# The two value blocks of a group put side by side behind the scores, over one stretch of a hybrid-attention decoder step

## The chip, the cores and the metric

The kernel runs on one core of a Trainium2 chip. The metric is the device time of one execution in microseconds, and the median of three executions stands for a kernel.

## What is computed

One decoder layer for 512 prompt tokens and for 8 sample sequences of 8 new tokens each. The part that matters here is the attention of the samples over stored keys and values: differential attention over 4096 paged positions in 4 heads, and dilated window attention over a stored window of 2048 positions in 8 heads.

```python
qa, ka, va, qb, kb, vb = _project(_rms_norm(xs, norm_attn_g[l]), w_in[l], pos_s)
k_past = cache_k_diff[l][page_table].reshape(db, PAST_LEN, N_HEADS_DIFF, 2, HEAD_DIM)
v_past = cache_v_diff[l][page_table].reshape(db, PAST_LEN, N_HEADS_DIFF, DIFF_V_DIM)
oa = _diff_attention_sample(qa, ka, va, k_past, v_past, lam)
ob, k_win, v_win = _dilated_attention_sample(qb, kb, vb, state_k_win[l], state_v_win[l])
...
s_past = jnp.einsum('bqhcd,bkhcd->bchqk', q, k_past, preferred_element_type=jnp.float32) * SCALE
p = jax.nn.softmax(jnp.concatenate([s_past, s_new], axis=-1), axis=-1)
w = p[:, 0] - lam * p[:, 1]
o = (jnp.einsum('bhqk,bkhe->bqhe', w[..., :p_len], v_past.astype(jnp.float32))
     + jnp.einsum('bhqk,bkhe->bqhe', w[..., p_len:], v_new.astype(jnp.float32)))
```

## The kernel before

The samples' attention is cut into 8 items of two sequences each. Items 0 to 3 read the paged cache, in 8 groups each; items 4 to 7 read the window state, in 3 groups each. That makes `KSLOTS` = 44 groups. A group is two halves (one for each sequence) of four pages of 128 keys; the third group of a state item has two pages a half. The program is one list of slots t = 0 to 52, each of eight steps i = 0 to 7, and every engine walks that list in its own program order. In slot t the keys of group t are scored, and the values of group t - 8 (`LAG` = 8) are weighed.

TensorE's part of a slot, before the change:

- i = 2: scores of half 0 (`score_keys`, line 1232, 16 matmuls into one PSUM bank);
- i = 4: turns the probabilities of group t - 8 (`turn_probs`, line 1245), which ScalarE then copies to `pt_sb` (line 1701); with the last group of an item also the scores of the new keys (line 1214);
- i = 5: values of half 0 (`weigh_values`, line 1270, 16 matmuls);
- i = 6: an item's new probabilities (line 1253) or its output (line 1329), then scores of half 1;
- i = 7: values of half 1, and an item's new values (line 1283).

Between these, each step has a share of the prompt's work (`pieces`): projection first, then the prompt's attention (lines 1084, 1099, 1115, 1132), and from slot 35 on the output projection (line 1189) with its transposes (line 1202). After slot 41 there is next to none of it until the prompt's second norm (line 1021).

VectorE transposes each key page from `k_ring` to `kt_sb` (`turn_page`, line 2175) once the scores of the page's half in the slot before have been made, and takes a slot's scores out of PSUM when both halves are there (`keep_scores`, line 2212). With an item's last group it then works out the bias (lines 2226 to 2243), and ScalarE makes the exponentials (line 1731). ScalarE also builds the next item's queries (`fetch_q`, lines 1686 and 1691), and for that it waits until all scores of the item before are made, half 1 of its last group included.

SyncE issues the loads in program order. `k_ring` holds one group of keys and `v_ring` one group of values. The load of value half h for slot t waits on `pv_half[h]`, which is the end of `weigh_values(t - 1, h)`. In SyncE's list the values of half 0 for slot t + 1 stand at i = 6 of slot t, one or two key loads behind them, and the values of half 1 at i = 0 of slot t + 1. From slot 44 on values go to three rings (`k_ring`, `v_ring`, `t_ring`), and ScalarE issues some of the loads.

Of the kernel before, what the change touches and what calls it, by code (L numbers as in the profile page):

```python
# [97 lines left out]
FIRST = [sum(QUADS[:it]) for it in range(ITEMS)]  # L98
KSLOTS = sum(QUADS)
# [7 lines left out]
def item_of(q):  # L107
    it = max(i for i in range(ITEMS) if FIRST[i] <= q)
    return it, q - FIRST[it]
# [7 lines left out]
def is_last(q):  # L117
    it, g = item_of(q)
    return g == QUADS[it] - 1


def has_k(t):
    return 0 <= t < KSLOTS


def has_v(t):
    return 0 <= t - LAG < KSLOTS
# [73 lines left out]
def pieces(t, i):  # L201
    return range(upto(t, i - 1), upto(t, i))
# [159 lines left out]
def build(nc, ins, outs):  # L362
    from contextlib import ExitStack
    ctx = ExitStack()
    with ctx:
# [643 lines left out]
        def _(pe):  # L1009
# [196 lines left out]
            def score_new_keys(it):  # L1206

                t0 = 4 * (it // 4)
                pe.wait_ge(rope_done, rope_no(8 if it < 4 else 20))
                pe.wait_ge(q_ready, it + 1)  # L1210
                if Z_NO["n", it]:
                    pe.wait_ge(z_free[1], Z_NO["n", it])
                for f in range(4):
                    last = nc.tensor.matmul(Z[1][32 * f:32 * f + 32, 0:NS], q_nat[:, f, :], k_s[:, t0 + f, :],
                                            start=True, stop=True)
                last.then_inc(z_full[1], 1)

            def score_keys(t, h):

                it, g = item_of(t)  # L1220
                n = pages_of(t)
                pe.wait_ge(kt_done, half_end(t, h))
                if g == 0:
                    pe.wait_ge(q_ready, it + 1)
                    pe.wait_ge(q_ready_dve, 1)
                if t and h == 0:
                    pe.wait_ge(s_evac, t)
                for r in range(4):
                    c0 = 32 * n * (2 * h + r // 2)
                    for f in range(4):  # L1230
                        c = 32 * (4 * f + r)
                        last = nc.tensor.matmul(S[32 * f:32 * f + 32, c0:c0 + 32 * n], q_st[:, h, f, r, :],  # L1232
                                                kt_sb[:, 4 * h:4 * h + n, c:c + 32], start=r % 2 == 0, stop=r % 2 == 1)
                last.then_inc(scored if h else half_scored, 1)

            def turn_probs(t):

                it, g = item_of(t - LAG)
                n = pages_of(t - LAG)
                pe.wait_ge(exp_done, EXP_NO[it, 4 * half_of(it, g) + 3] + 1)  # L1240
                if X_NO["p", t]:
                    pe.wait_ge(x_free, X_NO["p", t])
                for k in range(4):
                    c = col0(it, g) + 32 * n * k
                    last = nc.tensor.transpose(X[0:32 * n, k * P:(k + 1) * P], s_sb[:, c:c + 32 * n], ident[:, :])  # L1245
                last.then_inc(x_full, 1)

            def turn_new_probs(t):

                it = item_of(t - LAG)[0]  # L1250
                pe.wait_ge(exp_done, EXP_NO[it, 8] + 1)
                pe.wait_ge(x_free, X_NO["m", t])
                nc.tensor.transpose(X[0:NS, 0:P], s_sb[:, mini0(it):mini0(it) + NS], ident[:, :]).then_inc(x_full, 1)

            def weigh_values(t, h):

                q = t - LAG
                it, g = item_of(q)
                rows = 32 * pages_of(q)
                pe.wait_ge(x_free, X_NO["p", t] + 1)  # L1260
                if g == 0 and h == 0 and it:
                    pe.wait_ge(o_scaled, it)
                ring = ring_of(t)
                landed = (k_landed, v_landed, t_landed)[ring]
                for k in range(pages_of(q)):
                    pe.wait_ge(landed[4 * h + k], V_LANDS[q, 4 * h + k])
                for b in range(4):
                    values = (k_ring[0:rows, 4 * h + b, :], v_ring[0:rows, h, b, :], t_ring[0:rows, h, b, :])[ring]
                    for f in range(4):
                        last = nc.tensor.matmul(O[32 * f:32 * f + 32, P * h:P * h + P], pt_sb[0:rows, 4 * f + b, :],  # L1270
                                                values[:, f * P:(f + 1) * P],
                                                start=g == 0 and b == 0 and h == 0, stop=False, skip_group_check=True)
                last.then_inc(pv_half[h], 1)
# [51 lines left out]
            def turn_output(it):  # L1325

                pe.wait_ge(o_scaled, it + 1)
                pe.wait_ge(x_free, X_NO["o", it])
                nc.tensor.transpose(X[:, 0:P], o_row[:, :], ident[:, :]).then_inc(x_full, 1)
# [9 lines left out]
            for t in range(SLOTS):  # L1339
                for i in range(8):  # L1340
                    if i == 4 and has_v(t):
                        turn_probs(t)
                    if i == 4 and has_k(t) and is_last(t):
                        score_new_keys(item_of(t)[0])
                    if i == 6 and has_v(t) and is_last(t - LAG):
                        turn_new_probs(t)
                    if i == 6 and has_v(t - 1) and is_last(t - 1 - LAG):
                        turn_output(item_of(t - 1 - LAG)[0])
                    for p in pieces(t, i):
                        main(p)  # L1350
                    if i % 4 == 2 and has_k(t):
                        score_keys(t, i // 4)
                    if i == 5 and has_v(t):
                        weigh_values(t, 0)
                    if i == 7 and has_v(t):
                        weigh_values(t, 1)
                        if is_last(t - LAG):
                            weigh_new_values(t)
                    if (t, i) == (KSLOTS + 1, 6):

                        pe.wait_ge(ones_set, 1)
                        pe.wait_ge(sq_s_done, 1)
                        pe.wait_ge(z_free[1], Z_NO["s", 4])
                        nc.tensor.matmul(Z[1][:, 0:4 * NS], ones[:, :], sub_sq_s[:, :, :].rearrange("p g t -> p (g t)"),
                                         start=True, stop=True).then_inc(z_full[1], 1)
                    if (t, i) == (KSLOTS + 5, 4):
                        pe.wait_ge(norm_s_done, 1)
                        pe.wait_ge(z_free[1], len(Z_NO))
                        pe.wait_ge(wo_in, 16 * 8)
                        sample_out(0)  # L1370
# [1296 lines left out]
```

## Time and profile before

| | |
|---|---|
| median of three executions | 1108.67 us (1107.43 to 1110.65) |
| the profiled execution | 1107.77 us |
| its span | 1106.0 us |
| TensorE busy in the span | 960.3 us (87%) |
| VectorE, ScalarE busy | 671.5 us (61%), 506.3 us (46%) |
| mean granted TensorE clock | 0.949 of full speed |
| bytes moved | 310.98 MB, 281 GB/s on average |

The profile is of one execution. A line such as "L1270" is a line of the program; a matmul of float32 operands shows as two records, so the 16 matmuls of one half are "x32". PE is TensorE, DVE is VectorE, ACT is ScalarE, SPq is SyncE's queue of issues. What stands in square brackets is the idle time ahead of an instruction and what ended it.

### The profile page before, as it was taken

The numbers are of one execution on the slowest core, as the hardware profiler recorded it, in microseconds if no ns is written. First come the engines' busy times: TensorE is split into PE (matmuls) and PEld (weight loads), VectorE is DVE, ScalarE is ACT, GpSimd is POOL, SyncE is SP. The second block draws the span as 40 slices with busy tenths as digits, with TensorE's granted clock in tenths as the row PEclk, the third lists the DMA queues.
The fourth block names the chain that finished last, engine by engine and source line by source line (L and its number), as shares of the span: only waits on it lengthen the run. The fifth ranks groups of instructions, "written<-read, shape, count | busy, mean of one in ns | idle before, by whom it ended". The sixth has DMA issues, their size and how long they took to land.

```text
span 1106.0 us, 29349 instructions
## 1 busy us (share of the span) xinstructions
PE 960.3 (87%) x11050; PEld 852.3 (77%) x11050; DVE 671.5 (61%) x1632; ACT 506.3 (46%) x1118; POOL 133.9 (12%) x69
## 2 busy tenths in 40 slices
PE   3989898998777778888788757899999999999996
PEld 3978787887665556667566544699999999999996
DVE  5389655675458896765255444888888888800004
ACT  6554443373124656655144163465555555711124
POOL 1322211111000010001121000000000000043331
PEclk9989999999988998896999888999999999999998
DMA  8699999999999999978988699368676868956542
GB/s 252 240 310 341 326 317 356 367 351 334 299 323 335 348 353 336 323 229 275 328 284 298 197 301 255 130 252 317 256 311 248 319 245 311 324 176 235 192 166 86
DMA packets 174933, 310.98 MB, mean 281 GB/s; under 512 B 13601, under 2 KB 87714, under 8 KB 173282
## 3 DMA queue, kind: packets, MB, share of 16 engines
q1 hardware_dynamic: 172898, 305.24, 80.7%
q10 hardware_dynamic: 1920, 4.20, 1.4%
q8 instruction: 74, 1.21, 0.5%
q14 instruction: 41, 0.34, 0.1%
HBM read 302.30 MB, written 73.92 MB: 340 GB/s over the span
## 4 chain that ended last, share of the span: by engine, by line
PE 31%; issue 30%; SPq 13%; DMA 12%; DVE 7%; ACT 5%; ACTq 0%; POOL 0%; DVEq 0%; POOLq 0%
PE ps L1383 11%; SPq L666 7%; DMA v_ring<-in_cache_v_diff 6%; PE ps L1038 5%; SPq L768 4%; PE ps L1232 4%; PE ps L1270 4%; DVE kt_sb L2175 2%; PE ps L1189 2%; DMA k_ring<-in_state_v_win 2%; PE ps L1115 1%; SPq L756 1%; DMA k_ring<-in_cache_k_diff 1%; DMA k_ring<-in_state_k_win 1%; ACT q_st L1686 1%
## 5 line engine op out<-in xcount | busy, mean ns | idle before, releaser
L2175 DVE STREAM_TRANSPOSE kt_sb<-k_ring 128x512 f32<-128x512 f32 x336 | 221.2, 692 | 95.1 <-DMA k_ring<-in_cache_k_diff 41.7
L1270 PE MATMUL ps<-v_ring,pt_sb 128*32 128x128 f32 (+1 forms) x2496 | 93.6, 295 | 73.2 <-DMA v_ring<-in_cache_v_diff 59.6
L1270 PEld LDWEIGHTS ps<-v_ring,pt_sb 128*32 128x32 f32 (+1 forms) x2496 | 72.1, 117 | 88.8 <-issue 74.8
L1038 PE MATMUL ps<-h_hi,w_hi 128*128 128x288 f32 x384 | 125.1, 326 | 2.3 <-DVE h_lo L2028 2.3
L1038 PE MATMUL ps<-h_lo,w_hi 128*128 128x288 f32 x384 | 115.7, 301 | 0.0
L1038 PE MATMUL ps<-h_hi,w_lo 128*128 128x288 f32 x384 | 115.3, 300 | 0.0
L1232 PE MATMUL ps<-kt_sb,q_st 128*32 128x128 f32 (+1 forms) x2816 | 95.8, 279 | 9.5 <-DVE q_st L2185 4.6
L989 POOL TENSOR_TENSOR c_lo<-c_raw,c_hi 128x1408 fp32r<-128x1408 f32 x14 | 46.7, 3336 | 434.9 <-ACT c_hi L1789 434.9
L1232 PEld LDWEIGHTS ps<-kt_sb,q_st 128*32 128x32 f32 x2816 | 72.1, 113 | 26.8 <-issue 18.5
L1038 PEld LDWEIGHTS ps<-h_hi,w_hi 128*128 128x128 f32 x384 | 74.8, 195 | 16.4 <-issue 13.8
L949 POOL TENSOR_TENSOR w_lo<-w_raw,w_hi 128x1024 fp32r<-128x1024 f32 x24 | 57.4, 2392 | 228.3 <-ACT w_hi L1500 228.3
L1701 ACT ACTIVATE pt_sb<-ps 128x512 f32<-128x512 f32 (+1 forms) x44 | 26.2, 595 | 128.0 <-PE ps L1245 128.0
L1383 PE MATMUL ps<-a_hi,c_hi 128*128 128x288 f32 x352 | 79.1, 296 | 0.2 <-POOL c_lo L989 0.2
L1320 PE MATMUL ps<-t_h,s_h 128*128 128x288 f32 x264 | 77.9, 295 | 1.2 <-ACT u L1782 1.2
L1383 PE MATMUL ps<-a_lo,c_hi 128*128 128x288 f32 x352 | 78.9, 295 | 0.0
L1383 PE MATMUL ps<-a_hi,c_lo 128*128 128x288 f32 x352 | 78.6, 294 | 0.0
L1320 PE MATMUL ps<-t_l,s_h 128*128 128x288 f32 x264 | 77.9, 295 | 0.0
L1320 PE MATMUL ps<-t_h,s_l 128*128 128x288 f32 x264 | 77.7, 294 | 0.0
L2314 DVE TENSOR_TENSOR s_l<-s_t,s_h 128x512 fp32r<-128x512 f32 x88 | 58.8, 689 | 28.4 <-ACT s_h L1753 18.1
L1038 PEld LDWEIGHTS ps<-h_lo,w_hi 128*128 128x128 f32 x384 | 74.9, 195 | 0.0
L1038 PEld LDWEIGHTS ps<-h_hi,w_lo 128*128 128x128 f32 x384 | 74.6, 194 | 0.0
L2466 DVE TENSOR_TENSOR x<-x,ps 128x512 f32 x7 | 4.8, 689 | 111.1 <-PE ps L1396 111.1
(240 smaller groups left out, 2288.2 us busy)
## 6 DMA issues: line engine op xcount, KB each, us to landing
k_ring<-in_cache_k_diff SPq DMA_DIRECT2D x256, 256.0 KB, 5.5
v_ring<-in_cache_v_diff SPq DMA_DIRECT2D x256, 256.0 KB, 5.5
out_k_win_sample<-in_state_k_win SPq DMA_DIRECT2D x32, 1020.0 KB, 8.3
out_v_win_sample<-in_state_v_win SPq DMA_DIRECT2D x32, 1020.0 KB, 8.3
k_ring<-in_state_k_win SPq DMA_DIRECT2D x32, 512.0 KB, 8.3
w_raw<-in_w_in SPq DMA_DIRECT2D x24, 512.0 KB, 6.6
g_raw<-in_w_gate SPq DMA_DIRECT2D x11, 1024.0 KB, 5.4
g_raw<-in_w_up SPq DMA_DIRECT2D x11, 1024.0 KB, 5.4
```

The lines of the kernel that those rows point to most:

```text
L666: queue.dma_start(dst, src).then_inc((k_landed, v_landed, t_landed)[ring][i], 16)
L768: sp.dma_start(k_ring[:, at_first:i + 1, :].squeeze(1) if at_first == i else k_ring[:, at_first:i + 1, :], src)\
L949: nc.gpsimd.tensor_tensor(w_lo[:, n % 3, :], w_raw[:, n % 3, :], w_hi[:, n % 2, :].bitcast(F32), ALU.subtract).then_inc(w_lo_done, 1)
L989: nc.gpsimd.tensor_tensor(c_lo[j][:, 0:width], c_raw[:, j, 0:width], c_hi[j][:, 0:width].bitcast(F32), ALU.subtract).then_inc(w_lo_done, 1)
L1038: last = nc.tensor.matmul(M[c][:, 0:HALF], wt, act[:, k, c * HALF:(c + 1) * HALF], start=k == 0 and at_first, stop=k == KT - 1 and act is ...
L1232: last = nc.tensor.matmul(S[32 * f:32 * f + 32, c0:c0 + 32 * n], q_st[:, h, f, r, :], kt_sb[:, 4 * h:4 * h + n, c:c + 32], start=r % 2 == ...
L1270: last = nc.tensor.matmul(O[32 * f:32 * f + 32, P * h:P * h + P], pt_sb[0:rows, 4 * f + b, :], values[:, f * P:(f + 1) * P], start=g == 0 ...
L1320: last = nc.tensor.matmul(ps[:, bank, 0:HALF], wt[:, k, :], act[:, k, :], start=j in (0, 1, 3) and k == 0 and at_first, stop=k == 3 and wt ...
L1383: last = nc.tensor.matmul(main_ps[:, 2 * bank + c, 0:HALF], wt[j][:, w], a_lo[:, pair, block, :] if low else a_hi[pair][:, block, :], star ...
L1701: nc.scalar.activation(pt_sb[r].rearrange("p m (k t) -> p k m t", k=4), X[r].rearrange("p (k m t) -> p k m t", k=4, t=DT), ACT.Copy).then_ ...
L2175: V.transpose(kt_sb[:, i, :], k_ring[:, i, :]).then_inc(kt_done, 1)
L2314: V.tensor_tensor(dst[:, :, :], src, high[:, :, :].bitcast(F32), ALU.subtract).then_inc(form_low, 1)
```

## The change

In slots 32 to 43, which are those in which keys of the window state are scored, `weigh_values(t, 0)` is called at i = 7 and no longer at i = 5. It then stands right in front of `weigh_values(t, 1)`, and both scores of the slot stand in front of both halves of values. The slots before 32 and from 44 on are as they were. No wait is edited.

```diff
                     if i % 4 == 2 and has_k(t):
                         score_keys(t, i // 4)
-                    if i == 5 and has_v(t):
+
+                    if i == (7 if FIRST[4] <= t < KSLOTS else 5) and has_v(t):
                         weigh_values(t, 0)
                     if i == 7 and has_v(t):
                         weigh_values(t, 1)
```

TensorE in slot 42, a slot that has no prompt work around its blocks (L1245 turns the probabilities, L1253 the new ones, L1232 scores half 1, L1270 are the values, L1283 the new values):

```order
 L1245 MATMUL ps<-ident,s_sb 64x128 x4
-L1270 MATMUL ps<-v_ring,pt_sb 32x128 x16
 L1253 MATMUL ps<-ident,s_sb 64x128
 L1232 MATMUL ps<-kt_sb,q_st 32x128 x16
-L1270 MATMUL ps<-v_ring,pt_sb 32x128 x16
+L1270 MATMUL ps<-v_ring,pt_sb 32x128 x32
 L1283 MATMUL ps<-v_s,ptm 32x128 x8
```

The values of half 0 moved behind the new probabilities and the scores of half 1, and the two value blocks are one run of 32 matmuls.

TensorE in slot 43, the last of the stretch, which ends in the first probabilities of slot 44 and its values from `k_ring`:

```order
 L1245 MATMUL ps<-ident,s_sb 128x128 x4
 L1214 MATMUL ps<-k_s,q_nat 32x64 x4
-L1270 MATMUL ps<-v_ring,pt_sb 32x128 x16
 L1329 MATMUL ps<-ident,o_row 128x128
 L1232 MATMUL ps<-kt_sb,q_st 32x64 x16
-L1270 MATMUL ps<-v_ring,pt_sb 32x128 x16
+L1270 MATMUL ps<-v_ring,pt_sb 32x128 x32
 L1245 MATMUL ps<-ident,s_sb 128x128 x4
 L1270 MATMUL ps<-k_ring,pt_sb 32x128 x32
```

The last scores of the program now follow the new keys' scores and the output transpose directly. On the other engines no instruction moved.

## Rows read from the trace of the kernel before

**Rows 1.** The page's shares of the chain that ended last, by engine.

```profile
PE 31%; issue 30%; SPq 13%; DMA 12%; DVE 7%; ACT 5%; ACTq 0%; POOL 0%; DVEq 0%; POOLq 0%
```

**Rows 2.** By stretch: length; PE, PEld, DVE, ACT, POOL busy; PEclk, DMA share, GB/s.

```profile
525.60:547.50 21.90, 14.24 (x167) 10.80 (x166) 3.86 (x13) 2.14 (x3) 2.36 (x1) 0.92 0.96 311
573.40:591.60 18.20, 13.26 (x184) 10.02 (x183) 6.37 (x23) 2.76 (x5) 4.70 (x2) 1.00 0.77 238
617.20:631.40 14.20, 8.86 (x156) 6.61 (x155) 5.44 (x22) 1.34 (x3) 0.00 (x0) 0.73 0.60 149
637.60:700.00 62.40, 42.36 (x660) 28.41 (x662) 32.33 (x74) 31.23 (x64) 0.00 (x0) 0.81 0.93 244
```

**Rows 3.** TensorE's waits, slots 32 to 43: total us, times, longest.

```profile
PE ps L1270 <- DMA v_ring<-in_cache_v_diff: 15.5, 6, 4.7
PE ps L1270 <- DMA v_ring<-in_state_v_win: 5.7, 3, 4.0
PE ps L1232 <- issue: 2.2, 1, 2.2
```

**Rows 4.** TensorE in order of time, slot 36: start, us, what, [idle before].

```profile
533.20 1.08 PE L1270 MATMUL ps<-v_ring,pt_sb 128*32 128x128 f32 x32 [2.99 <-DMA v_ring<-in_cache_v_diff]
...
541.55 1.75 PE L1270 MATMUL ps<-v_ring,pt_sb 128*32 128x128 f32 x32 [4.67 <-DMA v_ring<-in_cache_v_diff]
```

**Rows 5.** TensorE, the end of slot 38 and slot 39.

```profile
569.46 1.06 PE L1270 MATMUL ps<-v_ring,pt_sb 128*32 128x128 f32 x32
...
581.20 1.08 PE L1270 MATMUL ps<-v_ring,pt_sb 128*32 128x128 f32 x32 [2.78 <-DMA v_ring<-in_cache_v_diff]
...
583.83 1.08 PE L1232 MATMUL ps<-kt_sb,q_st 128*32 128x128 f32 x32
...
587.07 1.08 PE L1270 MATMUL ps<-v_ring,pt_sb 128*32 128x128 f32 x32 [2.16 <-DMA v_ring<-in_cache_v_diff]
```

**Rows 6.** TensorE, slots 41 to 44.

```profile
604.83 1.08 PE L1232 MATMUL ps<-kt_sb,q_st 128*32 128x128 f32 x32 [0.70 <-DVE kt_sb L2175]
...
622.91 1.21 PE L1270 MATMUL ps<-v_ring,pt_sb 64*32 64x128 f32 x32 [4.05 <-DMA v_ring<-in_state_v_win]
...
627.63 1.93 PE L1270 MATMUL ps<-v_ring,pt_sb 64*32 64x128 f32 x32 [1.29 <-DMA v_ring<-in_state_v_win]
...
634.21 1.08 PE L1270 MATMUL ps<-v_ring,pt_sb 128*32 128x128 f32 x32 [0.31 <-ACT pt_sb L1701]
...
635.48 0.65 PE L1232 MATMUL ps<-kt_sb,q_st 128*32 128x64 f32 x32
...
646.78 3.64 PE L1270 MATMUL ps<-k_ring,pt_sb 128*32 128x128 f32 x64 [8.59 <-ACT pt_sb L1701]
```

**Rows 7.** SyncE's value issues in slots 38 to 42, one key load between.

```profile
566.80 3.67 SPq L666 DMA_DIRECT2D v_ring<-in_cache_v_diff  x4
571.29 0.59 SPq L768 DMA_DIRECT2D k_ring<-in_state_k_win  x1
572.08 4.55 SPq L666 DMA_DIRECT2D v_ring<-in_cache_v_diff  x4
...
610.45 1.16 SPq L666 DMA_DIRECT2D v_ring<-in_state_v_win  x2
...
615.25 1.12 SPq L666 DMA_DIRECT2D v_ring<-in_state_v_win  x2
...
624.16 8.00 SPq L666 DMA_DIRECT2D v_ring<-in_state_v_win  x8
```

**Rows 8.** From issue to landing: all value loads, slots 32 to 43; then those of 615.25.

```profile
DMA to landing us min/median/max: 3.8/8.4/12.8
...
DMA to landing us min/median/max: 11.4/11.6/11.7
```

**Rows 9.** ScalarE builds item 6's queries, between slots 40 and 41.

```profile
599.96 4.24 ACT L1686 ACTIVATE q_st<-q_s 32x64 f32<-32x64 f32 x16 [1.73 <-issue]
604.21 0.52 ACT L1691 ACTIVATE q_nat<-q_s 64x64 f32<-64x64 f32 x2
```

## The prediction

> **What bounds the kernel now.** I read the page's chain first: TensorE's own work and issue hold most of it, but SyncE's issues and the DMAs hold a quarter together [rows 1]. Then the busy time by stretch: the rows are slots 36 (from 525.6), 39 (573.4) and 42 (617.2), and what follows slot 43. In slots 36 and 39 TensorE is busy 14.2 of 21.9 us and 13.3 of 18.2 us, in slot 42 8.9 of 14.2 us, while DMA is at 0.96, 0.77 and 0.60 of its time [rows 2]. Then TensorE's waits over slots 32 to 43: 21.2 us in front of the value blocks, for loads, and 2.2 us once in front of the scores of a new item [rows 3]. So the stretch is a chain of load round trips: a value block ends, its ring half is free, SyncE issues the next load, it lands some 8 us later (3.8 to 12.8) [rows 8], the next slot's block runs.
>
> In a slot with a wait the value block of half 1 decides, not that of half 0. In slot 36 half 0 waited 2.99 us, and later TensorE still stood 4.67 us before half 1's values [rows 4]. Slot 39 has 2.78 and 2.16 us [rows 5], slot 42 4.05 and 1.29 us [rows 6]. In the slots between it waits little or not at all for loads, and its total work counts.
>
> **What the change removes and adds.** No work. In twelve slots a block of 1.08 us changes places with the prompt pieces and the scores of half 1 (1.08 us, or 0.65 in two-page groups) [rows 5, 6].
>
> **Waits in front of half 0.** They total 2.99 + 2.78 + 4.05 = 9.82 us. I value their removal at nothing by itself: what runs in them now would only make the wait in front of half 1's values longer. In slot 39 TensorE reaches the first wait at 581.20 - 2.78 = 578.42. The new probabilities, six pieces and the scores then take what they took between 582.2 and 584.9, so they end near 581.2; values 0 follow to 582.3; values 1 still start when their load has landed, at 587.07 [rows 5]. The wait becomes 4.8 us, and the slot ends where it did. The lower bound is the whole 9.82 us gained, which would need half 1's load to come sooner too; the upper is zero.
>
> **Half 0's loads are issued later.** Their release moves to just before the block of half 1. In slot 38 that is from 566.80 to about 569.6, or 2.8 us [rows 5, 7]. On SyncE the key load and half 1's issues stand behind: 4 issues took 3.67 us, the key load 0.59, so half 1's issues start near 569.6 + 3.7 + 0.6 = 573.9 in place of 572.08, 1.8 us late [rows 7]. In slots where the wait for half 1 is long (36, 39, 42 into the next) half 0's block ends well ahead of half 1's, and nothing is added. So the delay is bounded by 0 and 1.8 us at a slot that is late for its load, and there are two that follow a busy slot: 36 and 39. 0 to 3.6 us. The loads were 8.4 us under way against 3.8 at best [rows 8], so some 4.6 us of that was standing behind earlier transfers; a load issued 1.8 us later has less in front of it. I take 0.5 us for both.
>
> The Trainium skill ("DMA: Bandwidth & Descriptors", Queues, rings and completion order) says that on each DMA engine the descriptors are taken in ring order. By it, a later issue behind a backlog costs nothing and both slots give 0; the long landings agree, but the DMA share of 0.77 in slot 39 [rows 2] says that the backlog was not on all engines.
>
> **Scores of half 1 come earlier.** The block of 1.08 us is no longer in front of them, so at an item's end ScalarE begins the next queries 1.08 us sooner. They take 4.24 + 0.52 us and end at 604.73; TensorE begins the scores of slot 41 at 604.83, having stood 0.70 us [rows 6, 9]. The page puts that wait down to VectorE; by the times it is the queries. All 0.70 us are gained, then TensorE's own work is next. Between slots 34 and 35 the same wait is 2.2 us [rows 3], of which at most 1.08 goes; but the slots ahead of it receive half 0's load later, as in slot 38, and I set 0.6 against it: 0.5 gained. At the third item end, slot 37, TensorE shows no wait: 0. Sum -1.2 us; bounds 0 and -1.8.
>
> **Slot 42.** The scores of half 1 in slot 41 are 1.08 us earlier too, so VectorE frees the key ring sooner and SyncE reaches half 1's issue at 615.25 sooner, by up to the same 1.1 us. That load takes 11.6 us with DMA half idle [rows 2, 8]. Half 0's, issued at 610.45 [rows 7], is later by the pieces and scores that now run first, about 2 us; it landed 12.5 us after its issue (622.91) and would land near 624.5, in time. I take 1.1 us earlier for 627.63, bounds 0 and -1.5.
>
> **Slot 43 and behind.** Half 0's load at 624.16 now waits for a block that starts near 624.5 and ends near 626.5: 2.3 us later, half 1's load 1 us sooner [rows 6, 7]. The last scores, at 635.48, lose the block and the 0.31 us in front of them: 1.4 us, and 2.5 us with the 1.1 above. They release the bias, the exponentials and then the copy for which TensorE waits 8.59 us at 646.78 [rows 6]. But behind it 62.4 us run with DMA at 0.93 [rows 2], and what was issued by 632 is no more than before. The stretch ends with its transfers. Of 2.5 us I take 0.3; the bounds are 0 and 2.5. These 0.3 us stand in place of the 1.1 and 1.2, which end in the same transfers: of the 2.3 us ahead of slot 43 I keep 1.0, as half 0's late issue leaves DMA idle while it was at 0.60 [rows 2].
>
> **Sum.** +0.5 for the late issues, -1.0 for slots 35, 41 and 42 together, -0.3 behind 43: -0.8 us. Against the profiled execution, 1107.77, this gives 1107.0. The median of the runs lies 0.9 us above that execution, so a median of 1107.9; I say 1108.0. About 0.3% (3.3 us) is what can be told from no change here.
>
> **Rival 1, the score chain is worth its full price (faster).** Queries sooner at 34, 40 (1.08 + 0.70), slot 42 and the last scores 2.5 us sooner, all carried to the end: -4.3 us, a median of 1104.4. For it: the 8.59 us wait on ScalarE and the wait in front of new items are the only ones not for loads, and the change shortens both. Against it: DMA at 0.93 behind slot 43.
>
> **Rival 2, the loads bunch (slower).** Place: SyncE's list from half 0's to half 1's issue. Price: up to 1.8 us on half 1's load after a busy slot, and then the whole slot is later, as the block of half 1 frees the next load. It decides once the delay exceeds what stood in the queue ahead. Two slots by 1.8 us, and slot 33 by half of one, 0.9, and the late load of half 0 in slot 43 with its 2.3 us less 1 us sooner, 1.3: 5.8 us, less the 0.7 of slot 41: +5.1, a median of 1113.8. For it: DMA is only at 0.77 in slot 39, so a later issue there can leave it idle. Against it: landings of 8.4 us and more.
>
> **Rival 3, one long wait in place of two (slower).** In slot 36 TensorE came out of 4.67 us idle and the same block took 1.75 us in place of 1.08; in slot 42, after 4.05 and 1.29 us, the second took 1.93 [rows 4, 6]. After 2.78 and 2.16 us in slot 39 it kept 1.08 [rows 5] and the granted clock of that stretch was 1.00, that is 2.4 GHz [rows 2]. The change joins those two into one of about 4.8 us. If the clock falls to 1.2 GHz there, the value block costs 0.67 and the pieces behind it about 1 us more: +1.7, in place of -0.8, so +0.9 and a median of 1109.6, inside what counts as no change.
>
> The Trainium skill ("TensorE: Matmul & The Clock Gate", HAM oscillation — how this bites in real kernels) warns of idle gaps at TensorE that a wait for a DMA leaves. By it, slot 39 would fall to the lower clock; slots 36 and 42 agree.
>
> **Chances.** The forecast 0.42, rival 3 0.18, rival 1 0.22, rival 2 0.18. Of rival 1, 0.18 lies beyond 0.3%, of rival 2 0.15; the unknown of the others, landings that shift by chance, puts 0.04 on each side. Faster 0.22, the same 0.59, slower 0.19. The range takes in rival 1's time and most of the way to rival 2's: 1103.5 to 1112.5; the forecast's own range, with rival 3, is 1105.5 to 1110.5.
>
> **What would show it.** Right: in slots 36, 39 and 42 one wait before the first or second value block about as long as both before, and the block of half 1 within 1 us of its place; scores of slot 41 without a wait; the 8.59 us wait begins earlier by about 1 us, the first block behind it up to 2.5 us earlier, and the sample's last value block not. Wrong: half 1's loads in slots 33, 36 or 39 land over 1.5 us later, the sum of waits at the value blocks grows well over 21.2 us (rival 2), or the output projection's first tile behind slot 43 moves by over 3 us.

## The result, and the profile after

The change makes the kernel slower. Its median over 22 executions is 1118.89 us (1110.11 to 1128.99); that of the kernel before, over 22 executions beside them, is 1111.03 us. The ratio is 1.007, with a 95% interval of 1.0052 to 1.0087, so some 7.8 us. The forecast was 1108.0 us, with 1112.5 as the upper end. Of the 10.9 us between, 2.4 belong to the base: the forecast was worked out against a median of 1108.67 us from three executions, and 22 have 1111.03. The other 8.5 us are the change's effect, forecast at -0.7 and measured at +7.8.

The profiled execution after took 1119.42 us, its span 1117.6 us, with a granted clock of 0.940. Of the 11.6 us between the two spans, 3.4 lie ahead of slot 32 (its first scores start at 468.2 before and 471.6 after) and 1.2 behind the last value block: no edit reaches there, so they are scatter. The 7.0 us between lie in the slots that the change edits and in what follows them; how much of that is scatter too, the experiments have to tell. First the page: TensorE's busy time and the chain by engine, to hold against [rows 1].

```profile
PE 965.9 (86%) x11050; PEld 857.3 (77%) x11050; DVE 671.6 (60%) x1632; ACT 505.4 (45%) x1118; POOL 133.9 (12%) x69
issue 30%; PE 29%; SPq 15%; DMA 15%; DVE 6%; ACT 4%; POOL 0%; ACTq 0%; DVEq 0%; POOLq 0%
```

TensorE has the same 11050 matmul records and is busy 5.6 us longer: it ran slower somewhere. SyncE's issues and the DMAs, a quarter of the chain before, hold 30% of it. TensorE's waits in front of and inside the value blocks of slots 32 to 43, from 471.5 to 654.6 us (total us, times, longest), against [rows 3]:

```profile
PE ps L1270 <- DMA v_ring<-in_cache_v_diff: 18.6, 9, 6.4
PE ps L1270 <- DMA v_ring<-in_state_v_win: 8.2, 2, 5.1
PE ps L1270 <- issue: 2.9, 1, 2.9
```

The waits for loads in front of value blocks were 21.2 us and are 26.8. That is the sum whose growth was named ahead as the mark of rival 2. (The 2.9 us put down to "issue" stand inside a value block of slot 35 and are not in this sum.) Half of the growth, 2.8 us, is in slot 42, 0.9 in slot 39 and 0.7 in slot 36. Slots 39 and 42 are those that became plainly longer. TensorE in slot 39, against [rows 5]:

```profile
583.13 1.08 PE L1232 MATMUL ps<-kt_sb,q_st 128*32 128x128 f32 x32
585.21 1.08 PE L1270 MATMUL ps<-v_ring,pt_sb 128*32 128x128 f32 x32 [1.00 <-DMA v_ring<-in_cache_v_diff]
591.11 1.94 PE L1270 MATMUL ps<-v_ring,pt_sb 128*32 128x128 f32 x32 [4.83 <-DMA v_ring<-in_cache_v_diff]
592.98 1.08 PE L1283 MATMUL ps<-v_s,ptm 64*32 64x128 f32 x16
...
597.65 0.65 PE L1232 MATMUL ps<-kt_sb,q_st 128*32 128x64 f32 x32
```

The wait in front of half 1 became one of 4.83 us, as the forecast had it, with 1.00 us left in front of half 0. The block behind it took 1.94 us in place of 1.08, the new values 1.08 in place of 0.64. The granted clock was 0.50 from 591.1 to 593.1 and 0.51 up to 595.5, that is the lower of its two levels; before, it was 1.00 from the scores to the end of the slot. From the start of half 1's values to the next slot's scores it is 6.54 us; before it was 591.64 - 587.07 = 4.57. TensorE in slots 41 to 44, against [rows 6]:

```profile
609.82 1.08 PE L1232 MATMUL ps<-kt_sb,q_st 128*32 128x128 f32 x32
...
622.12 1.08 PE L1232 MATMUL ps<-kt_sb,q_st 128*32 128x128 f32 x32
...
630.91 1.93 PE L1270 MATMUL ps<-v_ring,pt_sb 64*32 64x128 f32 x32 [5.10 <-DMA v_ring<-in_state_v_win]
635.90 1.93 PE L1270 MATMUL ps<-v_ring,pt_sb 64*32 64x128 f32 x32 [3.06 <-DMA v_ring<-in_state_v_win]
...
654.54 3.64 PE L1270 MATMUL ps<-k_ring,pt_sb 128*32 128x128 f32 x64 [6.83 <-ACT pt_sb L1702]
```

The 0.70 us in front of slot 41 are gone, as forecast, and the wait at `k_ring`'s first block is 6.83 us in place of 8.59. But slot 42 waits 5.10 and 3.06 us where it waited 4.05 and 1.29. Half 1's values begin 13.8 us behind the slot's first scores; before it was 627.63 - 617.23 = 10.4. Half 0's begin 8.8 us behind them in place of 5.7. By stretch (columns as in [rows 2]), slot 39 and slot 42:

```profile
576.69:597.65 20.96, 15.14 (x185) 11.45 (x184) 6.40 (x23) 2.74 (x5) 4.68 (x2) 0.84 0.77 233
622.12:639.66 17.54, 8.61 (x154) 6.68 (x153) 5.47 (x22) 1.31 (x3) 0.00 (x0) 0.71 0.57 144
```

Slot 39 is 2.7 us longer with its clock at 0.84 in place of 1.00, slot 42, from scores to scores, 3.4 us longer at about the same DMA rate (144 against 149 GB/s).

### The profile page after: what moved, and what is told of

The parts are those of the page before. It is cut to its first block, busy times and chain, and to the rows that moved or that the text cites. A ratio compares the mean times of both kernels' runs of the same rounds, so it can differ in the third digit from the quotient of the medians.

```text
span 1117.6 us, 29349 instructions
## 1 busy us (share of the span) xinstructions
PE 965.9 (86%) x11050; PEld 857.3 (77%) x11050; DVE 671.6 (60%) x1632; ACT 505.4 (45%) x1118; POOL 133.9 (12%) x69
## 4 chain that ended last, share of the span: by engine, by line
issue 30%; PE 29%; SPq 15%; DMA 15%; DVE 6%; ACT 4%; POOL 0%; ACTq 0%; DVEq 0%; POOLq 0%
PE ps L1384 11%; SPq L666 7%; DMA v_ring<-in_cache_v_diff 6%; PE ps L1038 5%; SPq L768 4%; PE ps L1270 4%; DMA k_ring<-in_state_k_win 3%; PE ps L1232 3%; DVE kt_sb L2176 3%; DMA k_ring<-in_cache_k_diff 2%; DMA k_ring<-in_state_v_win 2%; ACT q_st L1687 1%; DMA v_ring<-in_state_v_win 1%; PE ps L1189 1%; SPq L756 1%
## 5 line engine op out<-in xcount | busy, mean ns | idle before, releaser
L1270 PE MATMUL ps<-v_ring,pt_sb 128*32 128x128 f32 (+1 forms) x2496 | 93.6, 295 | 76.3 <-DMA v_ring<-in_cache_v_diff 58.8
L1270 PEld LDWEIGHTS ps<-v_ring,pt_sb 128*32 128x32 f32 (+1 forms) x2496 | 73.1, 117 | 91.0 <-issue 81.5
L1232 PE MATMUL ps<-kt_sb,q_st 128*32 128x128 f32 (+1 forms) x2816 | 100.1, 287 | 8.3 <-DVE q_st L2186 4.6
L1232 PEld LDWEIGHTS ps<-kt_sb,q_st 128*32 128x32 f32 x2816 | 75.0, 116 | 26.3 <-issue 18.3
L1038 PEld LDWEIGHTS ps<-h_hi,w_hi 128*128 128x128 f32 x384 | 73.9, 192 | 16.1 <-issue 13.8
L2315 DVE TENSOR_TENSOR s_l<-s_t,s_h 128x512 fp32r<-128x512 f32 x88 | 58.8, 689 | 28.3 <-ACT s_h L1754 18.1
```

The source lines that it names most:

```text
L1038: last = nc.tensor.matmul(M[c][:, 0:HALF], wt, act[:, k, c * HALF:(c + 1) * HALF], start=k == 0 and at_first, stop=k == KT - 1 and act is ...
L2315: V.tensor_tensor(dst[:, :, :], src, high[:, :, :].bitcast(F32), ALU.subtract).then_inc(form_low, 1)
```

## Why slot 42: the release of a slot two places ahead

In the trace it starts in slot 40. SyncE's issues there (start, us, tile, times) before:

```profile
597.66 2.57 SPq L666 DMA_DIRECT2D v_ring<-in_state_v_win  x4
...
601.33 3.38 SPq L666 DMA_DIRECT2D v_ring<-in_state_v_win  x4
604.75 3.80 SPq L768 DMA_DIRECT2D k_ring<-in_state_k_win  x4
```

And after, down to slot 42's own value loads:

```profile
605.64 3.43 SPq L666 DMA_DIRECT2D v_ring<-in_state_v_win  x4
...
609.75 2.71 SPq L666 DMA_DIRECT2D v_ring<-in_state_v_win  x4
612.51 2.60 SPq L768 DMA_DIRECT2D k_ring<-in_state_k_win  x4
617.70 1.16 SPq L666 DMA_DIRECT2D v_ring<-in_state_v_win  x2
619.61 0.58 SPq L768 DMA_DIRECT2D k_ring<-in_state_k_win  x1
620.24 1.12 SPq L666 DMA_DIRECT2D v_ring<-in_state_v_win  x2
```

Slot 40 starts at 591.64 before and at 597.65 after. Half 0's values are issued 6.0 us behind that start before, 8.0 us after, and the two halves' loads, with the key loads behind them, are one burst. In the six us from that point of the slot the DMA engines, by stretches of 2 us (the last two columns are DMA share and GB/s), did this before:

```profile
597.64:599.64 2.00, 2.00 (x39) 1.46 (x43) 1.71 (x2) 0.59 (x2) 1.82 (x1) 1.00 0.61 190
599.64:601.64 2.00, 2.00 (x52) 1.67 (x41) 1.97 (x11) 1.61 (x7) 0.58 (x1) 1.00 0.92 329
601.64:603.64 2.00, 2.00 (x11) 1.57 (x10) 1.76 (x9) 1.92 (x8) 0.00 (x0) 1.00 0.92 320
```

and this after:

```profile
603.65:605.65 2.00, 2.00 (x78) 1.64 (x81) 1.10 (x10) 1.40 (x6) 1.82 (x1) 1.00 0.23 92
605.65:607.65 2.00, 2.00 (x36) 1.59 (x26) 1.79 (x8) 1.92 (x8) 0.57 (x1) 1.00 0.35 65
607.65:609.65 2.00, 2.00 (x12) 1.63 (x10) 2.00 (x5) 1.90 (x9) 0.00 (x0) 1.00 0.64 198
```

That is 1.68 MB against 0.71 MB: about 1 MB is late, and no one waits for it in slot 40 or 41, where TensorE is at its own work. It has to be moved all the same, and it stands in front of the loads of slot 42. From issue to landing these took 11.4 to 11.8 us before. After, they took:

```profile
DMA to landing us min/median/max: 12.4/13.6/15.0
```

They are two-page loads. At that time the two-page keys of slot 43 are loaded as well. Once only these two kinds are left, the DMA share is about a quarter, as if four of the sixteen engines worked. The stretches of 2 us from 2 us into slot 42 on, before:

```profile
619.20:621.20 2.00, 0.00 (x0) 0.00 (x0) 1.07 (x2) 0.77 (x2) 0.00 (x0) 1.00 0.24 54
621.20:623.20 2.00, 0.29 (x12) 0.32 (x16) 0.96 (x6) 0.00 (x0) 0.00 (x0) 1.00 0.26 81
623.20:625.20 2.00, 2.00 (x48) 1.40 (x41) 0.00 (x0) 0.27 (x1) 0.00 (x0) 0.63 0.31 109
```

and after:

```profile
626.10:628.10 2.00, 0.00 (x0) 0.00 (x0) 1.25 (x2) 0.00 (x0) 0.00 (x0) 1.00 0.27 100
628.10:630.10 2.00, 0.00 (x0) 0.00 (x0) 1.16 (x4) 0.00 (x0) 0.00 (x0) 0.87 0.24 62
630.10:632.10 2.00, 1.19 (x24) 1.22 (x28) 1.24 (x10) 0.00 (x0) 0.00 (x0) 0.50 0.27 88
632.10:634.10 2.00, 0.74 (x16) 0.29 (x8) 0.00 (x0) 0.00 (x0) 0.00 (x0) 0.50 0.26 92
```

Before, this slow part begins 2 us into the slot and lasts some 6 us; after, it begins 4 us into the slot and lasts 8.

The packets of the traces say which loads are slow. By the code a row of a two-page key load is 2 KB and one of a two-page value load 8 KB. The 2 KB packets run about four at a time, at a share of 0.25 to 0.29, also while many 8 KB packets run beside them at a share of up to 0.9. So it is the keys that keep to four places, and the last of the values wait among them. This train of narrow key loads runs from 610.7 to 625.6 us before and from 618.8 to 634.4 us after. Counted from slot 42's first scores it starts 6.5 us ahead before and 3.3 us ahead after, and ends 8.4 and 12.3 us behind. It is about as long as it was; it starts later.

The Trainium skill ("DMA: Bandwidth & Descriptors", Queues, rings and completion order) says that one DMA copy is split over at most sixteen rings, not always all of them; the share of 0.24 to 0.31 agrees.

## The experiments

Fifteen kernels, each timed beside the kernel before. For each trace I measured every slot from TensorE's first scores of the slot to the first of the next. "43" runs to the first value block from `k_ring`, "tail" from there to the samples' last value block. One execution each, us; they scatter. In the sections below an edit is shown by its added lines alone, against the kernel before, in e11_warm39 and e13_warm18 against the kernel after.

| kernel | ratio | 95% | 32 to 38 | 39 | 40 | 42 | 43 | tail |
|---|---|---|---|---|---|---|---|---|
| before | 1 | | 105.2 | 18.2 | 13.2 | 14.2 | 15.4 | 45.7 |
| after | 1.0070 | 1.0052 to 1.0087 | 105.0 | 21.0 | 12.2 | 17.5 | 14.9 | 48.4 |
| e1_first | 0.9995 | 0.9970 to 1.0019 | 106.4 | 20.5 | 13.2 | 13.9 | 15.2 | 47.5 |
| e2_last | 1.0031 | 1.0006 to 1.0057 | 106.0 | 22.0 | 12.2 | 17.8 | 14.9 | 53.1 |
| e3_delay | 1.0009 | 0.9981 to 1.0036 | 106.6 | 19.2 | 13.2 | 16.4 | 15.1 | 53.3 |
| e4_order5 | 1.0025 | 0.9997 to 1.0053 | 105.8 | 18.7 | 12.5 | 15.1 | 15.3 | 50.1 |
| e5_only41 | 1.0010 | 0.9982 to 1.0039 | 104.9 | 18.6 | 13.2 | 15.2 | 15.1 | 45.1 |
| e6_not41 | 1.0065 | 1.0030 to 1.0101 | 108.9 | 21.6 | 12.2 | 18.7 | 14.4 | 47.2 |
| e7_delay41 | 1.0011 | 0.9983 to 1.0039 | 105.8 | 19.6 | 13.2 | 13.7 | 15.4 | 47.1 |
| e8_again | 1.0062 | 1.0030 to 1.0095 | 107.5 | 22.2 | 12.2 | 16.7 | 14.2 | 46.4 |
| e9_not40 | 1.0048 | 1.0017 to 1.0080 | 106.4 | 22.6 | 13.2 | 15.2 | 14.9 | 48.7 |
| e10_delay40 | 1.0035 | 1.0001 to 1.0069 | 104.7 | 18.6 | 13.2 | 17.7 | 15.4 | 46.3 |
| e11_warm39 | 1.0085 | 1.0052 to 1.0117 | 108.7 | 21.9 | 12.2 | 18.3 | 14.4 | 45.4 |
| e12_ends | 0.9998 | 0.9971 to 1.0025 | 106.2 | 18.8 | 12.5 | 15.1 | 15.6 | 48.0 |
| e13_warm18 | 1.0059 | 1.0029 to 1.0088 | 106.6 | 20.5 | 12.2 | 17.2 | 14.9 | 50.7 |
| e14_not3940 | 1.0030 | 0.9993 to 1.0067 | 107.9 | 19.6 | 13.2 | 15.4 | 14.9 | 51.1 |
| e15_only3940 | 1.0068 | 1.0034 to 1.0103 | 106.6 | 21.0 | 12.2 | 18.1 | 16.8 | 47.8 |

Slot 41 took 12.0 to 13.1 us in all of them.

### Which slots, and which part of the move

The change in slots 32 to 38 alone:

```diff
+                    if i == (7 if FIRST[4] <= t < 39 else 5) and has_v(t):
```

> The change in slots 32 to 38 only. Late-load theory (half 0's load is issued later and half 1's load then lands late, above all where a load of two pages a half is slow anyway): little here, 0 to +2 us, as slots 33 to 38 gained and lost between -4.6 and +3.5 us in the two traces and stood 0.1 us earlier at the start of slot 39, seen from slot 32. Clock theory (two waits joined into one): one such slot, 36, slow before too, so 0 to +1 us. If the loss is spread evenly over the slots, as a cost of the order itself: 7 of 12 slots, about +4.5 us.

The change in slots 39 to 43 alone:

```diff
+                    if i == (7 if 39 <= t < KSLOTS else 5) and has_v(t):
```

> The change in slots 39 to 43 only. Late-load theory: nearly the whole loss, +5 to +8 us, most of it in slot 42 (+3.4 us in the trace) and behind slot 43. Clock theory: slot 39 alone, +2 to +3 us, and nothing in slot 42, where the clock was low before. Even spread: about +3 us.

The first half of the stretch costs nothing that can be told (0.9995), the second does (1.0031, less than the 5 to 8 us that the late-load theory expected), and it carries both long slots, 39 and 42.

TensorE's order of before, and in SyncE's list, in front of half 0's value issue, a wait for the scores of half 1 of the same slot. That is about when the change releases the load:

```diff
+                        if t >= FIRST[4]:
+                            sp.wait_ge(scored, t + 1)
```

> TensorE's order as before; only SyncE's issue of half 0's values, for slots 33 to 43, waits until half 1's scores of the slot before are made. Late-load theory: +4 to +8 us, as in the change. Clock theory: near 0, since the scores still stand between the two waits; at most +1 us. If the order itself costs: 0.

TensorE's other half of the move: the scores of half 1 at i = 5, ahead of the values of half 0, which stay at i = 5:

```diff
+                    if i == (5 if FIRST[4] <= t < KSLOTS else 6) and has_k(t):
+                        score_keys(t, 1)
```

> Both scores of a slot ahead of both values, in slots 32 to 43, but by moving the scores of half 1 forward to step 5: half 0's values move back by 1.08 us only, and stay apart from half 1's. Late-load theory: 0 to +1.5 us, or faster by 1 to 2 us as the queries of the next item start sooner. Clock theory: 0 to +1 us. If the order of scores before values itself costs: +5 us or more.

Neither shows the loss of 0.7% (1.0009 and 1.0025, both intervals reach below 1). The late-load theory had expected 4 to 8 us of e3_delay and missed. The late release in every slot does not lengthen slot 39 as the changed order does (19.2 us), so rival 2 falls at slot 39. Slot 36, its other main place, took 25.2 us there against 21.9 before and stays open (see **Open** below). And it lengthens slot 42, to 16.4 us.

### Slot 41, a theory that fell

The nearest cause for slot 42 is the release in slot 41, which is where its half 0 comes from. Three kernels: the change in slot 41 alone, everywhere else, and SyncE's wait there alone.

```diff
+                    if i == (7 if t == 41 else 5) and has_v(t):
```

> The change in slot 41 alone, so that the two-page value load of half 0 for slot 42 is released about 2 us later than before, and within 3 us of half 1's. Shared-engines theory (the two-page loads of both halves run on the same few DMA engines at a quarter of the DMA share, and only their distance kept the second from standing behind the first): slot 42, from its first scores to slot 43's, goes from 14.2 to about 17.5 us, and the kernel is 2 to 4 us slower. Clock theory: slot 42 as before. Even spread over the slots: +0.6 us.

```diff
+                    if i == (7 if FIRST[4] <= t < KSLOTS and t != 41 else 5) and has_v(t):
```

> The change in slots 32 to 43 without slot 41, where half 0's values stay ahead of half 1's scores. Shared-engines theory: slot 42 back to about 14 us, though it has the new order itself, and the kernel 3 to 4 us faster than with the whole change, so +0.3 to +0.5% against before. Clock theory: still +0.6 to +0.7%. Even spread: +0.64%.

```diff
+                        if t == 41:
+                            sp.wait_ge(scored, t + 1)
```

> TensorE's order as before everywhere; SyncE holds back half 0's value load for slot 42 alone until half 1's scores of slot 41 are made. Shared-engines theory: slot 42 at 16 to 17.5 us, +2 to +3 us in all. Theories that go by TensorE's order or clock: 0.

The change once more, beside them:

> The changed kernel once more, for a second trace and more times. Shared-engines theory: slot 42 at 17 to 18 us again. Slot 39 at 20 to 22 us against 18.2 (before) and 20.5 (change in the first seven slots only), and the stretch from the first block on k_ring to the last value block anywhere from 45 to 53 us, as it was in six traces without a pattern. Time +0.6 to +0.8%.

Slot 42 takes 15.2 and 13.7 us where slot 41 alone is changed or late, and 18.7 us where all but 41 is changed. The release in slot 41 is not the cause. The repeat gave 1.0062.

### Slot 40, and the clock in slot 39

The change everywhere but in slot 40:

```diff
+                    if i == (7 if FIRST[4] <= t < KSLOTS and t != 40 else 5) and has_v(t):
```

> The change in slots 32 to 43 without slot 40. The four profiles with the change in slots 39 and 40 had slot 42 at 16.7 to 18.7 us, those without at 13.7 to 15.2; slot 41 alone did nothing. Theory now: half 0's value load for slot 41, released in slot 40, comes 3 us later, lies in one burst with half 1's, and the two-page loads for slots 42 and 43, which run on a few DMA engines at a quarter of the share, start behind it. Then slot 42 is at 14 to 15 us and the kernel 3 us faster than the whole change, at +0.3 to +0.5%. If slot 42 is late because of its own order, it stays at 17 to 18 us, and the kernel at +0.65%.

The late release in slot 40 alone, in TensorE's order of before:

```diff
+                        if t == 40:
+                            sp.wait_ge(scored, t + 1)
```

> TensorE's order as before; SyncE holds back half 0's value load for slot 41 alone until half 1's scores of slot 40 are made. Burst theory: slot 42 at 16 to 18 us, +2 to +3 us in all. Own-order theory: slot 42 at 14 us, time as before.

These two settle where slot 42's length comes from. With TensorE's order untouched, one wait on SyncE in slot 40 makes slot 42 17.7 us long, and its value loads land late. The kernel was 0.35% slower, with an interval that begins at 0.01%. SyncE's issues, TensorE's blocks, the two stretches of slot 40 and the landing, in e10_delay40 (its lines 1234 and 1272 are 1232 and 1270 of before):

```profile
599.77 3.53 SPq L666 DMA_DIRECT2D v_ring<-in_state_v_win  x4
...
603.97 2.99 SPq L666 DMA_DIRECT2D v_ring<-in_state_v_win  x4
```

```profile
617.09 1.08 PE L1234 MATMUL ps<-kt_sb,q_st 128*32 128x128 f32 x32
626.04 1.93 PE L1272 MATMUL ps<-v_ring,pt_sb 64*32 64x128 f32 x32 [7.32 <-DMA v_ring<-in_state_v_win]
...
630.99 1.93 PE L1272 MATMUL ps<-v_ring,pt_sb 64*32 64x128 f32 x32 [0.80 <-DMA v_ring<-in_state_v_win]
```

```profile
599.49:601.49 2.00, 2.00 (x52) 1.67 (x41) 1.97 (x11) 1.60 (x7) 0.61 (x1) 1.00 0.46 125
601.49:603.49 2.00, 2.00 (x10) 1.57 (x10) 1.76 (x9) 1.92 (x8) 0.00 (x0) 1.00 0.65 169
```

```profile
DMA to landing us min/median/max: 14.6/14.8/15.1
```

The issue came 2.1 us later, at the same place of the slot the DMAs moved 125 and 169 GB/s in place of 329 and 320, the train of narrow key loads starts 3.3 us ahead of slot 42 in place of 6.5, and the value block of half 1 begins 13.9 us behind the scores in place of 10.4. With slot 40's order restored (e9_not40) the loads of slot 42 landed in

```profile
DMA to landing us min/median/max: 9.7/11.4/13.1
```

and the slot took 15.2 us; the train starts over 6 us ahead of it again. The whole kernel was still 0.48% slower, with slot 39 at 22.6 us.

That slot 42's 3 us reach the kernel's time is less well shown. e3_delay holds the same wait in slot 40, with slot 42 at 16.4 us, and its time can't be told from before (1.0009, up to 1.0036).

For slot 39 the question is how much of its length is the clock. The change, with 34 matmuls by the identity into a bank that nobody reads, between the two value blocks of slot 39:

```diff
+                    if (t, i) == (39, 7):
+                        pe.wait_ge(z_free[0], UNITS)
+                        pe.wait_ge(ones_set, 1)
+                        for n in range(34):
+                            nc.tensor.matmul(ps[:, 3, 0:P], ones[:, :], ident[:, :], start=True, stop=True)
```

> The changed kernel with 34 extra matmuls of 128 columns in slot 39, in the wait between half 0's and half 1's values, into a PSUM bank that nobody reads then (about 4 us of work in a wait of 4.8 to 5.1 us). Clock theory: the granted clock stays at 1.00 there, half 1's values take 1.08 and not 1.94 us, what follows them up to slot 40's scores takes 4.6 and not 6.5 to 7.4 us, and the kernel is 2 to 3 us faster than the change, at +0.4 to +0.5% against before. If the clock is not what slot 39 lost: 0 or a little slower than the change.

The same with `range(18)`:

> As the run with 34 extra matmuls in slot 39, with 18 of them: the 34 took 7.9 us, 3 us more than the wait, so they gave back what the clock saved; 18 take 4.2 us and fit. Clock theory: half 1's values at 1.08 us, slot 39 at 18.5 to 19.5 us against 21 to 22.6, kernel 2 to 3 us faster than the change, +0.4 to +0.5% against before. If the clock is not the loss of slot 39: slot 39 stays above 21 us.

TensorE in e11_warm39:

```profile
583.95 7.86 PE L1360 MATMUL ps<-ident,ones 128*128 128x128 f32 x68
591.74 1.08 PE L1270 MATMUL ps<-v_ring,pt_sb 128*32 128x128 f32 x32
...
596.31 0.66 PE L1232 MATMUL ps<-kt_sb,q_st 128*32 128x64 f32 x32
```

and in e13_warm18:

```profile
586.56 1.08 PE L1270 MATMUL ps<-v_ring,pt_sb 128*32 128x128 f32 x32 [2.39 <-DMA v_ring<-in_cache_v_diff]
587.57 4.29 PE L1360 MATMUL ps<-ident,ones 128*128 128x128 f32 x36
592.57 1.08 PE L1270 MATMUL ps<-v_ring,pt_sb 128*32 128x128 f32 x32 [0.72 <-DMA v_ring<-in_cache_v_diff]
...
597.12 0.65 PE L1232 MATMUL ps<-kt_sb,q_st 128*32 128x64 f32 x32
```

Where TensorE had work in the wait, half 1's block took 1.08 us and the next scores came 4.57 and 4.55 us behind its start, as before the change. In the six unwarmed traces with slot 39 changed (after, e2, e6, e8, e9, e15) it took 1.93 or 1.94 us behind waits of 4.83 to 5.34 us, and the next scores came 6.5 to 7.6 us behind its start. Half 1's block itself is not later there: it begins 14.5 us into the slot in the mean of those six and 14.4 in the nine that keep the order of values in slot 39. So what slot 39 loses lies behind the block: the joined wait costs the clock, and the clock costs 2.0 to 3.0 us. That filling the wait wins this back in the kernel's time isn't shown. In e11 the 7.86 us of extra matmuls are longer than the wait that they fill, and the kernel was 0.85% slower; in e13 half 0's load was late by itself, the slot took 20.5 us and not the 18.5 to 19.5 expected, and 1.0059 lies inside the change's interval.

### The earlier scores alone, and slots 39 and 40 alone

The scores of half 1 at i = 5 only in the last slots of items, which is where the next queries wait for them:

```diff
+                    if i == (5 if t in (34, 37, 40, 43) else 6) and has_k(t):
+                        score_keys(t, 1)
```

> A version that should keep the one gain of the change: slots 40 and 43 were 1.0 and 0.7 us shorter with it, as the scores that the next queries and the last exponentials wait for are made sooner. Here only the last scores of items 4 to 7 (slots 34, 37, 40 and 43) move, forward to step 5 ahead of half 0's values, which are then held back by those scores alone (0.65 us in the trace). If the gain can be had so: 1 to 2.5 us faster than before, -0.1 to -0.2%, at the edge of what can be measured. If the next slots give it back to the loads: no change.

This keeps most of what the forecast hoped for, with slot 40 at 12.5 us, and leaves slots 39, 41 and 42 in their order. It is no faster than before (0.9998): 0.7 us can't be told.

The change without slots 39 and 40, and in these two alone:

```diff
+                    if i == (7 if FIRST[4] <= t < KSLOTS and t not in (39, 40) else 5) and has_v(t):
```

> The change in slots 32 to 38 and 41 to 43, not in 39 and 40. If the joined wait of slot 39 and the late load released in slot 40 are the two causes: slot 39 at 18.5 to 20.5, slot 42 at 14 to 15.5 us, the kernel within 0.25% of before. If the order costs everywhere: +0.5%.

```diff
+                    if i == (7 if t in (39, 40) else 5) and has_v(t):
```

> The change in slots 39 and 40 alone. Two-causes theory: slot 39 at 21 to 22.5 us, slot 42 at 17 to 18.5, slot 40 a microsecond shorter, +4 to +6 us in all, +0.35 to +0.55%. If the order costs everywhere: +0.1%.

The two slots alone give 1.0068, with 21.0 and 18.1 us for slots 39 and 42; without them the kernel stands at 1.0030, with an interval that holds 1, and with 19.6 and 15.4 us. Both times lie above what was expected of them (0.35 to 0.55%, and at most 0.25%). TensorE in e15_only3940 shows both causes, the block at half clock and the late loads of slot 42:

```profile
590.40 1.94 PE L1270 MATMUL ps<-v_ring,pt_sb 128*32 128x128 f32 x32 [5.10 <-DMA v_ring<-in_cache_v_diff]
...
597.62 0.65 PE L1232 MATMUL ps<-kt_sb,q_st 128*32 128x64 f32 x32
...
632.20 1.93 PE L1270 MATMUL ps<-v_ring,pt_sb 64*32 64x128 f32 x32 [7.67 <-DMA v_ring<-in_state_v_win]
```

## Why the prediction was wrong

**The sizes.** From the table, as means over the traces with and without the change in the slot concerned:

| place | with | without | difference, us |
|---|---|---|---|
| slot 39 (changed there, unwarmed: 6; order of values as before: 9) | 21.7 | 19.1 | +2.6 |
| slot 40 (changed: 7; not, and scores at i = 6: 8) | 12.2 | 13.2 | -1.0 |
| slot 42 (slot 40 changed: 7; as before there in both lists: 6, without e4 and e12) | 17.8 | 14.6 | +3.2 |
| slots 32 to 38 (changed: 8; not: before, e2, e5, e7, e10, e15) | 107.2 | 105.5 | +1.7 |
| slot 43 (changed: 8; not: before, e1, e5, e7, e10; with e15's 16.8 the mean is 15.6) | 14.7 | 15.3 | -0.6 |

The three rows of slots 39, 40 and 42 make +4.8 us, 0.43%. Their ranges of slots 39 and 42 do not overlap between the groups (21.0 to 22.6 against 18.2 to 20.5; 16.7 to 18.7 against 13.7 to 15.4). This agrees with the timings, as far as they can tell: the change at 1.0070 less e14 at 1.0030 is 0.40%, and e15's interval of 0.34 to 1.03% holds it.

**What bounds the kernel: right in kind.** The stretch is a chain of load round trips with half 1's block as the one that decides. What it missed is that a slot without a wait also hands on a debt: slots 40 and 41 never wait for a load, and the late traffic of slot 40 is paid in slot 42.

**Waits in front of half 0, valued at nothing: right for slot 39's load, not for the slot.** There the wait in front of half 1 was put at 4.8 us and is 4.83. But "the slot ends where it did" failed: the slot is 2.7 us longer, 2.0 of it behind the wait, where the clock was at its lower level (the other 0.8 ahead of half 1's values). That term was put at nothing in the sum, though rival 3 had named it. In slots 36 and 42 the two waits did not become one: they are 2.0 and 6.4 us, and 5.10 and 3.06 us.

**Scores of half 1 earlier, -1.2 us: right at slot 41,** where the 0.70 us are gone and slot 40 is 1.0 us shorter in every trace with the change there. At slots 34 and 35 nothing can be told: slots 32 to 38 together are 0.1 us shorter in the profiled execution, and 1.7 us longer in the means.

**The step that failed: "Slot 42".** It said that half 1's value block would come 1.1 us earlier, from "That load takes 11.6 us with DMA half idle", and that half 0's would land "in time". The block comes 3.4 us later (13.8 against 10.4 us into the slot) in place of 1.1 us earlier, and the slot is 3.4 us longer. Half 0's block was put near 624.5, 7.3 us into the slot, and comes at 8.8. The 11.6 us were taken for a property of the load. They hold its place behind the narrow key loads and the traffic of the slots before, and became 12.4 to 15.0 us once slot 40's burst stood in front. The forecast priced the late release of half 0 only at the next slot (0 to 3.6 us, taken as 0.5) and only where TensorE then waits. In slot 39 this held, by e3_delay. In slot 40, which it did not look at, as it priced only slots that are late for their loads, the DMA engines had less to do for lack of an issue, and this was worth 3.2 us in slot 42.

The prediction set beside its 0.5 us the rule of the Trainium skill (in the section named above) that descriptors are taken in ring order, and drew from it that a late issue behind a backlog is free. The trace does not contradict the rule: at slot 40 there is no backlog, with a share of 0.23 in the 2 us ahead of the issue.

**Rival 2** is thus right in its mechanism (a late issue leaves the DMA idle, and the loads bunch), but its main cost came at a place that it did not have: the two-page loads two slots on, not half 1's load in slots 33 and 39. At slot 36 it is not refuted (see below). That its time of 1113.8 us lies nearest to the measured one is in part luck: 3.2 us of its kind are shown, at a place that isn't in its sum of +5.1. It had 0.18.

**Rival 3 was right in its place and its cause, and too small:** 1.7 us forecast for slot 39, 2.6 measured. What was missing is that the new values (1.08 against 0.64 us) and the pieces behind run at the lower clock too, 6.5 to 7.6 us in place of 4.57; the rival had put the pieces at 1 us. It also should not have stood beside the forecast as an alternative. It does not exclude the rest of the sum, and its +2.6 and rival 2's +3.2 came together. The Trainium skill's warning ("TensorE: Matmul & The Clock Gate", HAM oscillation — how this bites in real kernels) about idle gaps that a DMA wait leaves agrees with 1.08 against 1.94 us.

**Slot 43 and behind, -0.3 us.** The stretch from slot 43's first scores to the block behind ScalarE's copy is 0.6 us shorter in the means, with 14.9 against 15.4 us in the two profiled executions. No gain behind it is seen: the tail takes 45.4 to 53.1 us with slot 43 changed and 45.1 to 47.8 us in the six without any edit that bears on slot 43 (before, e1, e5, e7, e10, e15); the means are 48.9 and 46.6.

**Open.** The three slots explain some 4.8 of 7.8 us. The rest would be the 1.7 us of slots 32 to 38 and the 2.3 us of the tail. The first is not borne out by the time of e1_first (0.9995, up to 1.0019), and yet slot 36 is not plain scatter. With slots 32 to 38 changed it took 22.5 to 30.7 us (mean 27.0), without 20.9 to 22.6 us (21.8). Most of this is waiting that moved: slots 32 to 35 together are 3.0 us shorter (54.5 against 57.5). Counted from slot 32's first scores, half 1's block of slot 36 begins at 72.6 to 77.4 us with the change and at 72.2 to 74.5 without, in the means 1.6 us later. That would be rival 2's 1.8 us at its own place; the ranges overlap, and no run here changes slots 35 and 36 alone. The tail scatters over 8 us, in kernels that don't change slot 43 too (e3_delay 53.3). No experiment here took the tail apart. Nor do the parts add up within their intervals to better than 0.3%: slots 39 to 43 gave 1.0031 and slots 39 and 40 alone 1.0068.

No version that was run is faster than the kernel before.

## What to carry to other kernels

A block that frees a buffer is also the start signal of a transfer. Before moving it later, look at the DMA share in the stretch in which its load would now be missing, and not only at whether anyone waits for that load: where the share is under one, the idle time can be a debt that the next slow load pays, slots later. A landing time that is read from a trace includes the queue in front of it and moves with it. Two waits that become one can cost the clock behind them, and that covers all work up to the point where it is back, not the block alone.

## What was not expected of the hardware

- Two-page value and key loads, alone in flight, ran with a DMA share of 0.24 to 0.31 at 54 to 109 GB/s for 6 to 8 us, against 0.9 and over 300 GB/s for four-page loads. It is the key loads' 2 KB packets that run four at a time; 8 KB packets of the value loads ran beside them at a share of up to 0.9.
- The granted clock stayed at 1.00 through waits of 2.78 and 2.16 us with blocks of 1.08 us and pieces between them [rows 5], and was halved after one wait of 4.83 us. The level is not decided by the wait alone: in e7_delay41 a wait of 2.49 us, with 2.36 us earlier in the slot, was followed by a block of 1.93 us, and in e14_not3940 a block of slot 39 still took 1.08 us behind a wait of 3.79 us.
- A matmul of float32 operands with 128 columns takes 0.23 to 0.24 us at full clock: 34 of them 7.86 us, 18 of them 4.29 us.
